# Eight of twelve modulation blocks of a two-layer diffusion step summed on VectorE instead of TensorE

## The chip, the core and the metric

One program on one core of a Trainium2 chip. The metric is the device time of one execution in microseconds (us), here as the median of several runs.

## What is computed

One inference step of a hybrid backbone with two layers over 128 context tokens (stream 0) and 256 latent tokens (stream 1), model width 1024, all in fp32. Per layer and stream (`silu`, `rmsnorm` and `softmax` as usual):

```
mod = silu(c) @ w_mod + b_mod             # 1024 -> 6144; stream 0 uses c_ctx instead of c
sh1, sc1, g1, sh2, sc2, g2 = split(mod, 6)
h = rmsnorm(x) * (1 + sc1) + sh1
z = h @ w_in                              # pooling input, q k v, latent q and kv, 3 x 1024 gates
merged = sum over 3 branches: sigmoid(gate_b) * (y_b @ w_br_b)
x = x + g1 * (merged @ w_out)             # y_b: windowed pooling, windowed GQA, latent attention
h = rmsnorm(x) * (1 + sc2) + sh2
x = x + g2 * moe(h)                       # 16 experts, each takes its top tokens; SwiGLU
```

## The kernel before

Every engine runs a program written out by hand, and semaphores alone tie them together. The 384 tokens are three tiles of 128 (`TILES` = 1, 2, 0). A layer is a mixing part and an expert part.

**Weights.** The mixing weights come as 57 units of 1 MB (`plan_units`), loaded by SyncE in a fixed order through a ring of 8 slots: a unit may be issued once the unit 8 places before it is used up (`wait_mixing`). Each of the 12 modulation blocks `i` (512 columns of `mod`) is two units, the halves of the 1024 rows of `w_mod`. The expert weights come as 96 double units of 2 MB per layer, through the same 8 slots and 8 more (eight doubles in all). The first three doubles go to slots 8 to 13, which lie over memory of the attention, after it (`load_early`, L537 issues every double); the next four wait for the last eight mixing units, and the eighth for the mixed `x`.

**Modulation.** `mod(l, i)` (L1476) is 8 products: the weight operand is `cs`, silu of the two conditions in 32 columns, and 512 columns of `w_mod` stream past; four such products take the four column groups of the array. Their result stands in rows 32q and 32q+1 of a bank and is copied to `modrow` or `g2slot` (`mod_row`, L716). For a block that is needed per channel, `mod_cols` (L1487) adds up the four groups and turns the block into columns by products with a two-column operand; VectorE adds the bias (L1014 to L1019). Blocks 0 to 3 are `sh1` and `sc1`, 4 and 5 `g1`, 6 to 9 `sh2` and `sc2`, 10 and 11 `g2`. `g1` and `g2` are wanted along the rows: one product with a 0/1 matrix spreads them over the partitions (L1737, L1804), and VectorE adds a broadcast bias that GpSimd's queue fetched (`gb`, `g2slot`).

**Mixing part, TensorE's order.** Blocks 0 to 3 and the input projection (L1591, L1627); block 6; transposes of q and k (L1638 to L1653); block 7; the latent query product (L1665) and pooling (L1671); blocks 8 and 9; then for four key tiles `t` the latent key/value product (L1692), and for three of them the transposes of a query tile (L1686); the column products of blocks 6 to 9; the transposes of the four key tiles (L1686); the first scores (L1511 to L1517). VectorE prepares each tile in `query(t)` and `key(t)` (L1214 to L1220); `key(2)` waits for the transposes of key tile 0, `key(3)` for those of tile 1. After `key(2)` VectorE computes amplitude and shift from blocks 6 to 9 and the router's weights (L1237 to L1241).

**Attention.** Eight head pairs `m`. Each turn of the loop on TensorE: `gate` (L1526, 8 products), `branch` (L1545, 4 products), transposes of one head's probabilities (L1554), `gate`, transposes of the other head's, the scores of the next pair, `branch`, `values` (L1566, L1569). ScalarE takes tanh of a gate (L755) and the exponentials; the branch product of the same step takes the gate's bank and so waits for that tanh. VectorE takes the maxima (L1057 to L1066), divides (L1075 to L1079), merges gate and branch (L1044, L1048) and copies (L1251). Then blocks 4 and 5, and eight steps of `gate(2, j)`, `branch(2, j)`.

**Output projection.** `project_out` (L1750) starts once all of `merged` is there; VectorE adds to `x` (`add_mixed`, L1277, L1281); transposes, router, top-k and numbering of tokens follow piece by piece; blocks 10 and 11 stand between the last of them; then the gather (L1815, L1826), evacuated by ScalarE and VectorE (L1388, L1390), the two rows of `g2` (L1804), and the expert part (L1880, L1917) as a loop over four groups of four experts.

## Time and profile before

| | |
|---|---|
| median of 3 runs | 1852.26 us (1850.01 to 1854.09) |
| the profiled execution | 1852.09 us, of which 1850.3 us are its span |
| busy share of the span | TensorE 94%, VectorE 27%, ScalarE 16%, GpSimd 6% |
| chain that ended last | TensorE 73%, DMA 22%, VectorE 2%, ScalarE 1% |
| expert part of layer 0 | 485.7 to about 932 us |
| expert part of layer 1 | 1400.5 us to the end |

A busy TensorE is not TensorE at its peak. The chain is followed back from the last instruction, at each step to what released it; "DMA" in it is time in which the last release was a transfer.

### The profile page before, as it was taken

The page shows a single profiled execution, that of the slowest core. Times are in us where ns is not written, and L with a number is a line of the kernel's source. Part 1 is how long each engine was busy: PE and PEld are TensorE (multiplying, and loading weights), DVE is VectorE, ACT ScalarE, POOL GpSimd, SP SyncE. Part 2 cuts the span into 40 slices and gives each one's busy share as a digit, 9 for nine tenths or more (in the row PEclk, how much of TensorE's full clock was granted, in tenths as well). Part 3 has the DMA queues.
Part 4 walks back from the last instruction along what each step waited for, and adds up shares of the span by engine and source line. Part 5 has one row for each costly group of instructions (what it writes and reads, how often), then busy time and mean ns, then how long its engine had stood idle before and what let it go on. Part 6 is the DMA issues. An engine that isn't in the chain of part 4 may idle for free.

```text
span 1850.3 us, 19029 instructions
## 1 busy us (share of the span) xinstructions
PE 1732.9 (94%) x7336; PEld 806.0 (44%) x7336; DVE 493.6 (27%) x1131; ACT 293.6 (16%) x737; POOL 115.2 (6%) x156
## 2 busy tenths in 40 slices
PE   6998999999999989898899989999999999988987
PEld 3455555554434333242245555555544343323322
DVE  1345333222312211121124344332132221201211
ACT  2233222101201010000022333221012010100100
POOL 1151000000000000000012410000000000000000
PEclk9998999999999999999999989999999999999999
DMA  9452111542999999999983701117419999999997
GB/s 385 182 217 93 69 69 69 207 179 80 381 429 431 431 431 431 431 431 429 428 359 117 278 24 68 69 69 282 172 58 430 429 431 431 431 431 431 430 431 323
DMA packets 48528, 531.77 MB, mean 287 GB/s; under 512 B 5776, under 2 KB 6832, under 8 KB 9808
## 3 DMA queue, kind: packets, MB, share of 16 engines
q1 hardware_dynamic: 45776, 524.45, 68.0%
q0 software_dynamic: 1536, 5.87, 0.9%
q8 instruction: 44, 0.72, 0.2%
q10 hardware_dynamic: 1152, 0.56, 0.1%
q14 instruction: 20, 0.16, 0.0%
HBM read 528.73 MB, written 2.13 MB: 287 GB/s over the span
## 4 chain that ended last, share of the span: by engine, by line
PE 73%; DMA 22%; DVE 2%; ACT 1%; issue 1%; SPq 0%; ACTq 0%; POOL 0%; DVEq 0%; POOLq 0%
PE bank L1880 20%; DMA ring<-in_w_moe 20%; PE bank L1526 13%; PE bank L1545 7%; PE bank L1591 6%; PE bank L1917 5%; PE bank L1750 5%; PE bank L1627 2%; DMA ring<-in_w_mix 2%; PE bank L1476 2%; PE bank L1815 2%; PE bank L1692 2%; PE bank L1554 1%; PE bank L1665 1%; PE bank L1569 1%; PE bank L1514 1%
## 5 line engine op out<-in xcount | busy, mean ns | idle before, releaser
L1526 PE MATMUL bank<-hT,ring 128*128 128x384 f32 x768 | 260.7, 493 | 0.0
L1880 PE MATMUL bank<-M,hT 128*64 128x512 f32 x1024 | 228.8, 595 | 20.4 <-DMA M<-in_w_moe 19.8
L1880 PE MATMUL bank<-ring,hT 128*64 128x512 f32 x1024 | 227.2, 595 | 11.1 <-DMA ring<-in_w_moe 11.1
L1526 PEld LDWEIGHTS bank<-hT,ring 128*128 128x128 f32 x768 | 144.0, 191 | 105.5 <-issue 12.5
L1880 PEld LDWEIGHTS bank<-M,hT 128*64 128x64 f32 x1024 | 73.0, 137 | 168.4 <-issue 137.4
L1545 PE MATMUL bank<-M,ring 128*128 128x384 f32 x384 | 134.2, 492 | 10.1 <-ACT M L755 10.1
L1880 PEld LDWEIGHTS bank<-ring,hT 128*64 128x64 f32 x1024 | 72.7, 137 | 157.5 <-issue 139.2
L1880 PE MATMUL bank<-ring,M 128*64 128x512 f32 x512 | 115.4, 596 | 18.7 <-DMA ring<-in_w_moe 18.7
L1880 PE MATMUL bank<-M 128*64 128x512 f32 x512 | 115.6, 595 | 12.3 <-DMA M<-in_w_moe 12.3
L1591 PE MATMUL bank<-ring,hT 128*128 128x512 f32 (+1 forms) x288 | 117.4, 567 | 2.8 <-DVE hT L1036 2.1
L937 ACT ACTIVATE hT<-bank 128x512 f32<-128x512 f32 x32 | 19.1, 597 | 574.6 <-PE bank L1880 574.6
L1545 PEld LDWEIGHTS bank<-M,ring 128*128 128x128 f32 x384 | 71.0, 190 | 67.9 <-ACT M L755 20.0
L1917 PE MATMUL bank<-M 128*128 128x512 f32 x192 | 93.8, 621 | 3.3 <-DVE M L1413 3.3
L1750 PE MATMUL bank<-ring,xn 128*128 128x512 f32 x192 | 85.5, 596 | 2.3 <-DVE xn L1048 2.3
L1400 DVE SCALAR_TENSOR_TENSOR hT<-hT,bank 128x512 f32<-128x512 f32 x32 | 22.0, 688 | 231.5 <-ACT hT L937 231.5
L1591 PEld LDWEIGHTS bank<-ring,hT 128*128 128x128 f32 x288 | 54.2, 190 | 63.6 <-issue 62.0
L597 POOL TENSOR_TENSOR rstd<-var,mhalf 128x8 f32<-128x8 f32 (+2 forms) x38 | 47.2, 1244 | 515.9 <-DVE var L960 515.8
L1405 DVE SCALAR_TENSOR_TENSOR hT<-hT,bank 128x512 f32<-128x512 f32 x32 | 22.0, 688 | 213.1 <-PE bank L1880 213.1
L1413 DVE TENSOR_TENSOR M<-bank,g2slot 128x512 f32<-128x512 f32 x32 | 22.1, 692 | 210.8 <-PE bank L1880 210.8
L1880 PEld LDWEIGHTS bank<-ring,M 128*64 128x64 f32 x512 | 36.8, 137 | 90.4 <-issue 77.8
L1424 DVE TENSOR_TENSOR x<-x,bank 128x512 f32<-128x512 f32 x96 | 66.0, 688 | 30.2 <-PE bank L1917 30.0
L1880 PEld LDWEIGHTS bank<-M 128*64 128x64 f32 x512 | 37.4, 137 | 83.2 <-issue 79.0
(224 smaller groups left out, 1483.3 us busy)
## 6 DMA issues: line engine op xcount, KB each, us to landing
M<-in_w_moe SPq DMA_DIRECT2D x96, 2048.0 KB, 31.5
ring<-in_w_moe SPq DMA_DIRECT2D x96, 2048.0 KB, 30.6
ring<-in_w_mix SPq DMA_DIRECT2D x110, 1024.0 KB, 7.1
ring<-in_w_mix SPq DMA_DIRECT2D x4, 576.0 KB, 4.5
M<-in_counts POOLq DMA_DIRECT2D x2, 768.0 KB, 12.4
out<-x SPq DMA_DIRECT2D x6, 256.0 KB, 2.0
x<-in_x_sample SPq DMA_DIRECT2D x1, 1024.0 KB, 8.2
M<-in_b_mod POOLq DMA_DIRECT2D x2, 512.0 KB, 7.7
```

The source lines that it names most:

```text
L597: nc.gpsimd.tensor_tensor(rstd[:, c0:c0 + n], var[:, c0:c0 + n], mhalf[:, 0:n], ALU.pow)\
L1424: V.tensor_tensor(xs, xs, bank[b][:, :], ALU.add).then_inc(bank_read[b], 1)
L1476: ins = mm(ps[32 * q:32 * q + 32, :], cs[:, 4 * h + q, :], w[:, q, :], start=(h == 0), stop=(h == 1))
L1526: ins = mm(ps[:, 0:TOK], w[:, q, (j % 4) * P:(j % 4 + 1) * P], hT[:, 4 * h + q, :], start=(h == 0 and q == 0), stop=(h == 1 and q == 3))
L1545: ins = mm(ps[:, 0:TOK], w[:, q, (j % 4) * P:(j % 4 + 1) * P], y[:, q, :], start=(q == 0), stop=(q == 3))
L1591: ins = mm(ps[:, 0:n], hT[:, 4 * h + q, t * P:(t + 1) * P], w[:, q, 0:n], start=(h == 0 and q == 0), stop=(h == 1 and q == 3))
L1627: ins = mm(ps[:, 0:TOK], w[:, q, g * P:(g + 1) * P], hT[:, 4 * h + q, :], start=(h == 0 and q == 0), stop=(h == 1 and q == 3))
L1692: ins = mm(ps[:, :], ckvT[:, k, t * P:(t + 1) * P], w[:, k, h * 512:(h + 1) * 512], start=(k == 0), stop=(k == 1))
L1750: ins = mm(ps[:, :], merged[:, kb, t * P:(t + 1) * P], w[:, kb % 4, :], start=(kb == 0), stop=(kb == 7))
L1815: mm(v[:, :, CP:USED], xn[:, t, kb * P:(kb + 1) * P], gsel[:, t, :].rearrange("p (e s) -> p e s", s=SLOTS)[:, :, CP:USED], start=(t == 1), ...
L1880: ins = mm(bank[b][64 * e:64 * e + 64, :], lhs(e, 4 * h + q), w[:, q, :], start=(h == 0 and q == 0), stop=(h == 1 and q == 3))
L1917: mm(bank[b][:, :], selT[:, t * P:(t + 1) * P], osb[:, n * 512:(n + 1) * 512], start=True, stop=True).then_inc(bank_full[b], 1)
```

## The change

Blocks 6, 7, 8, 9, 4, 5, 10 and 11 (`SUMMED`) are no longer products. VectorE goes over each unit of `w_mod` where it lies in the ring: for each of its four row blocks `q` and each stream `s` it multiplies the 512 columns by `cs[:, kb, s]`, one number per partition, and adds to an accumulator in `modrow` (even blocks) or `g2slot` (odd blocks), 8 instructions per unit and 16 units per layer (`sum_rows`). What is left is the sum over partitions: for blocks 6 to 9 eight products with a single column of ones (`column`, on TensorE), for `g1` and `g2` products of a matrix of ones or of 0/1 slot masks with the accumulators (`modb`, `gate_row`); the bias of these four is loaded into the accumulator beforehand (zero but for partition 0), and VectorE's bias additions and the halving of `g1` move into ScalarE's copy. The four bias loads stand on GpSimd's queue, each behind the product that read the accumulator's last contents; the sum that follows waits for its load. The units stand in a new order, and SyncE waits for `mod_summed` where it waited for a product. The router's weights move into step 1 of the last gate loop. `values(m)` moves behind the first gate of the next pair, except before pair 4. The transposes of the key tiles now follow the last key/value product directly. The output projection waits for `merged` block by block. The mixing part still has 57 units, the expert part is the same.

```diff
 def plan_units():
...
-    for i in (6, 7):
-        units += [("mod", i, 0), ("mod", i, 1)]
-    units += [("wq", 0, 0), ("wq", 1, 0)]
-    for i in (8, 9):
-        units += [("mod", i, 0), ("mod", i, 1)]
-    units += [("wkv", 0, 0)]
...
+    units += [("wq", 0, 0), ("wq", 1, 0), ("wkv", 0, 0)]
+    for b in range(2):
         for h in range(2):
-            units += [("gate", (b, h), 0), ("gate", (b, h), 1), ("br", (b, h), 0)]
-    for n in range(2):
-        units += [("wo", n, 0), ("wo", n, 1)]
-    for i in (10, 11):
-        units += [("mod", i, 0), ("mod", i, 1)]
+            i = 6 + 2 * b + h
+            units += [("mod", i, 0), ("gate", (b, h), 0), ("gate", (b, h), 1), ("br", (b, h), 0), ("mod", i, 1)]
+    units += [("gate", (2, 0), 0), ("gate", (2, 0), 1), ("br", (2, 0), 0), ("mod", 4, 0), ("mod", 4, 1), ("mod", 5, 0),
+              ("gate", (2, 1), 0), ("gate", (2, 1), 1), ("br", (2, 1), 0), ("mod", 5, 1)]
+    units += [("mod", 10, 0), ("mod", 10, 1), ("wo", 0, 0), ("wo", 0, 1), ("mod", 11, 0), ("mod", 11, 1), ("wo", 1, 0),
+              ("wo", 1, 1)]
...
-AFTER_ATTENTION = NU - RING - 1
+AFTER_ATTENTION = UNIT_AT["gate", (2, 1), 1]
...
+SUMMED = (6, 7, 8, 9, 4, 5, 10, 11)
+BIASED = SUMMED[4:]
...
             def wait_mixing(l, u):
 
-                if u in FIRST_AT:
+                if u[0] == "mod" and u[1] in SUMMED:
+                    sp.wait_ge(mod_summed, 2 * len(SUMMED) * l + SUM_AT[u[1], u[2]])
+                elif u in FIRST_AT:
...
-                wait_full(pool, l, ("o", NM - 1))
-                pool.dma_start(gb, a["b_mod"][l, 2 * D:3 * D].partition_broadcast(P)).then_inc(gate_row_in, 16)
-                pool.dma_start(g2slot[:, :], a["b_mod"][l, 5 * D:6 * D].partition_broadcast(P)).then_inc(gate_row_in, 16)
+                for n, i in enumerate(BIASED):
+                    wait_full(pool, l, ("col", 8 + n) if n < 2 else ("modb", BIASED[n - 2], 1))
+                    dst = modrow[:, :, :].rearrange("p s c -> p (s c)") if i % 2 == 0 else g2slot[:, :]
+                    pool.dma_start(dst, a["bias_rows"][l, n]).then_inc(bias_in[n], 16)
...
+                def sum_rows(i, h, qs):
+
+                    u = ("mod", i, h)
+                    w = unit_view(u)
+                    if 0 in qs:
+                        if h == 0 and i in BIASED:
+                            dve.wait_ge(bias_in[BIASED.index(i)], 16 * (l + 1))
+                        dve.wait_ge(*unit_landing(l, u))
+                    for q in qs:
+                        kb = 4 * h + q
+                        for s in range(2):
+                            acc = part_sum(i, s)
+                            if kb:
+                                dve.wait_ge(part_summed, parts[0] - 1)
+                            parts[0] += 1
+                            if kb or i in BIASED:
+                                ins = V.scalar_tensor_tensor(acc, w[:, q, :], cs[:, kb, s:s + 1], acc, ALU.mult, ALU.add)
+                            else:
+                                ins = V.tensor_scalar(acc, w[:, q, :], cs[:, kb, s:s + 1], None, ALU.mult)
+                            ins.then_inc(part_summed, 1)
...
                 for m in range(NM):
                     for j in range(2):
                         divide(l, m, j)
+                    if m in (3, 5, 7):
+                        column(6 + (m - 3) // 2)
                     merge(l, m // 4, 2 * m % 8)
                     for j in range(2):
...
+                        if j == 0:
+                            sum_rows(6 + m // 2, m % 2, (0, 1))
                     if m + 1 < NM:
                         maxima(l, m + 1, 0)
                     merge(l, m // 4, 2 * m % 8 + 1)
                     if m + 1 < NM:
                         maxima(l, m + 1, 1)
+                    sum_rows(6 + m // 2, m % 2, (2, 3))
...
                 for j in range(KB):
                     merge(l, 2, j)
+                    if j == 1:
+                        column(9)
+                        router_weights()
+                    else:
+                        i, h = {0: (4, 0), 2: (4, 1), 3: (5, 0), 4: (5, 1), 6: (10, 0), 7: (10, 1)}.get(j, (0, 0))
+                        if i:
+                            sum_rows(i, h, range(4))
...
                 add_mixed(0, 1)
+                sum_rows(11, 0, (0, 1))
                 add_mixed(1, 1)
+                sum_rows(11, 0, (2, 3))
                 add_mixed(0, 2)
                 turned(1, 1)
                 x_variance(1)
+                sum_rows(11, 1, (0, 1))
                 add_mixed(1, 2)
...
                 affinities(1)
+                sum_rows(11, 1, (2, 3))
                 add_mixed(0, 0)
...
+                def column(i):
+
+                    ps = begin(l, ("col", i))
+                    pe.wait_ge(mod_summed, 2 * len(SUMMED) * l + SUM_AT[i, 1])
+                    for s in range(2):
+                        for c in range(4):
+                            ins = mm(ps[:, 2 * c + s:2 * c + s + 1], part_sum(i, s)[:, c * P:(c + 1) * P], ones[:, 0:1],
+                                     start=True, stop=True)
+                    done(l, ("col", i), ins)
...
                     gate(l, b, j)
+                    if m not in (0, 4):
+                        values(l, m - 1)
+                    if m in (3, 5, 7):
+                        column(6 + (m - 3) // 2)
                     branch(l, b, j)
...
                     branch(l, b, j + 1)
-                    values(l, m)
...
                         if kb % 4 == 0:
                             arrived(l, ("wo", n, kb // 4))
+                        if n == 0 and t == TILES[0]:
+                            pe.wait_ge(merged_ready, 24 * l + 16 + kb + 1)
...
-                pe.wait_ge(merged_ready, 24 * (l + 1))
...
-                mod(l, 10)
+                for k in range(2):
+                    gate_row(10, k)
                 turn_x(0, 1)
-                mod(l, 11, (0,))
+                gate_row(11, 0)
                 router(0)
-                mod(l, 11, (1,))
+                gate_row(11, 1)
...
-                gate_row(10)
-                gate_row(11)
```

Three places of the order, as the program issues them (layer 0).

TensorE, from pooling to the first scores. Before (L1476 the blocks, L1692 the key/value product, L1686 transposes of query and key tiles, L1487 the columns of blocks 6 to 9):

```order
L1671 MATMUL bank<-M 128x384 x4
L1476 MATMUL bank<-ring,cs 32x512 x16
L1692 MATMUL bank<-ring,M 128x512 x4
L1686 MATMUL bank<-const,M 96x128 x8
...
L1692 MATMUL bank<-ring,M 128x512 x4
L1487 MATMUL bank<-const,modrow 128x2 x8
L1487 MATMUL bank<-const,g2slot 128x2 x8
L1686 MATMUL bank<-const,M 96x128 x32
L1511 MATMUL bank<-kT,M 128x128 x2
L1514 MATMUL bank<-kT,M 128x384 x2
```

Of the change (L1725 is L1671, L1744 is L1692, L1738 is L1686, L1567 is L1511):

```order
L1725 MATMUL bank<-M 128x384 x4
L1744 MATMUL bank<-ring,M 128x512 x4
...
L1744 MATMUL bank<-ring,M 128x512 x4
L1738 MATMUL bank<-const,M 96x128 x32
L1567 MATMUL bank<-kT,M 128x128 x2
```

Blocks 8 and 9 and the columns are gone, and the last product is followed by the key transposes.

TensorE, the second head pair. Before (L1526 gate, L1545 branch, L1566 and L1569 values of the first pair):

```order
L1566 MATMUL bank<-M 64x128 x2
L1569 MATMUL bank<-M 64x256 x6
L1526 MATMUL bank<-hT,ring 128x384 x8
L1545 MATMUL bank<-M,ring 128x384 x4
L1554 MATMUL bank<-const,M 128x128 x7
L1526 MATMUL bank<-hT,ring 128x384 x8
```

Of the change (L1582 gate, L1601 branch, L1622 and L1625 values):

```order
L1582 MATMUL bank<-hT,ring 128x384 x8
L1622 MATMUL bank<-M 64x128 x2
L1625 MATMUL bank<-M 64x256 x6
L1601 MATMUL bank<-M,ring 128x384 x4
L1610 MATMUL bank<-const,M 128x128 x7
```

The values of the first pair now stand between the gate of the second pair and its branch.

VectorE, from the last maxima of the second pair to the first copy of transposed probabilities. Before:

```order
L1064 TENSOR_SCALAR negm<-mx,negsink 128x3
L1075 TENSOR_TENSOR esink<-esink,rsum 128x3
L1077 RECIPROCAL rinv<-esink 128x3
L1079 TENSOR_SCALAR M<-M,rinv 128x128
L1079 TENSOR_SCALAR M<-M,rinv 128x384 x2
...
L1044 SCALAR_TENSOR_TENSOR xn<-M,bank 128x384
L1251 COPY M<-bank 128x384 x2
```

Of the change (L1076 is L1064, L1091 is L1079, L1305 is L1251; L1287 is the new sum):

```order
L1076 TENSOR_SCALAR negm<-mx,negsink 128x3
L1287 SCALAR_TENSOR_TENSOR modrow<-ring,cs,modrow 128x512 x4
L1087 TENSOR_TENSOR esink<-esink,rsum 128x3
L1089 RECIPROCAL rinv<-esink 128x3
L1091 TENSOR_SCALAR M<-M,rinv 128x128
L1091 TENSOR_SCALAR M<-M,rinv 128x384 x2
...
L1056 SCALAR_TENSOR_TENSOR xn<-M,bank 128x384
L1305 COPY M<-bank 128x384
L1287 SCALAR_TENSOR_TENSOR modrow<-ring,cs,modrow 128x512 x4
L1305 COPY M<-bank 128x384
```

Four sums of block 6 stand ahead of the division, four more between the two copies.

## Rows read from the trace of the kernel before

**Rows 1.** The chain in order of time: start us, us, what
```profile
485.72 20.82 PE bank L1880 x96
...
883.68 33.36 DMA ring<-in_w_moe
...
1400.50 20.82 PE bank L1880 x96
...
1798.58 33.36 DMA ring<-in_w_moe
```

**Rows 2.** SyncE's queue, four expert loads around the first expert product
```profile
473.35 23.25 SPq L537 DMA_DIRECT2D M<-in_w_moe  x4
```

**Rows 3.** ScalarE in order of time, layer 0: start us, us, instruction [idle before]
```profile
111.51 0.38 ACT L798 ACTIVATE M<-bank 128x256 f32<-128x256 f32 x1
113.08 0.60 ACT L716 ACTIVATE modrow<-bank 128x512 f32<-128x512 f32 x1 [1.19 <-PE bank L1476]
```

**Rows 4.** TensorE in order of time: three places of layer 0
```profile
133.74 3.64 PE L1476 MATMUL bank<-ring,cs 128*32 128x512 f32 x32
...
382.08 5.32 PE L1526 MATMUL bank<-hT,ring 128*128 128x384 f32 x16
...
389.82 5.32 PE L1526 MATMUL bank<-hT,ring 128*128 128x384 f32 x16
```

**Rows 5.** The chain: transposes behind the key projections, layers 0 and 1
```profile
155.46 3.47 PE bank L1487 x32
...
1071.14 4.04 PE bank L1487 x32
```

**Rows 6.** TensorE in order of time: first scores of layers 0 and 1
```profile
170.35 0.80 PE L1511 MATMUL bank<-kT,M 64*128 64x128 f32 x4 [0.88 <-ACT M L851]
...
1086.85 0.80 PE L1511 MATMUL bank<-kT,M 64*128 64x128 f32 x4 [0.88 <-ACT M L851]
```

**Rows 7.** VectorE in order of time, the third key tile of layer 0
```profile
156.90 0.17 DVE L960 TENSOR_SCALAR var<-ss 128x8 f32<-128x8 f32 x1
160.54 0.88 DVE L1214 TENSOR_TENSOR M<-bank,rstd 128x256 f32<-128x256 f32 x2 [3.47 <-PE bank L1686]
...
162.18 0.42 DVE L1220 TENSOR_TENSOR M<-krg,rstd 128x256 f32<-128x256 f32 x1
```

**Rows 8.** Stretch of 2 us, TensorE alone: busy, granted clock, DMA share, GB/s
```profile
171.00:173.00 2.00, 2.00 (x10) 0.50 0.00 0
```

**Rows 9.** TensorE in order of time, from the second head pair to the third
```profile
217.03 1.47 PE L1569 MATMUL bank<-M 128*64 128x256 f32 x12
...
224.43 2.85 PE L1545 MATMUL bank<-M,ring 128*128 128x384 f32 x8 [0.58 <-ACT M L755]
...
227.12 0.93 PE L1554 MATMUL bank<-const,M 128*128 128x128 f32 x7
```

**Rows 10.** TensorE at the start and the end of the output projection's stage
```profile
422.24 7.99 PE L1750 MATMUL bank<-ring,xn 128*128 128x512 f32 x18 [1.16 <-DVE xn L1048]
...
483.50 1.94 PE L1804 MATMUL bank<-modrow,const 128*128 128x512 f32 x4
```

**Rows 11.** VectorE in order of time, before the last tile's output projection
```profile
458.08 0.23 DVE L1316 TENSOR_SCALAR M<-M 128x16 f32<-128x16 f32 x1
...
459.62 0.69 DVE L1277 TENSOR_TENSOR M<-bank,M 128x512 f32<-128x512 f32 x1 [1.30 <-PE bank L1750]
```

**Rows 12.** VectorE, the last gathered rows before the experts of layer 0
```profile
484.86 0.40 DVE L1390 TENSOR_SCALAR hT<-bank,amp,shift 128x128 f32<-128x128 f32 x1
```

**Rows 13.** Groups by line and shape: instructions, busy us, mean ns, idle before
```profile
L1281 DVE TENSOR_TENSOR x<-x,M 128x512 f32<-128x512 f32 x12 | 8.3, 692 | 0.4
```

**Rows 14.** VectorE in order of time, between the second and third head pair
```profile
219.86 0.23 DVE L1064 TENSOR_SCALAR negm<-mx,negsink 128x3 f32<-128x3 f32 x1
...
220.40 0.95 DVE L1079 TENSOR_SCALAR M<-M,rinv 128x128 f32<-128x128 f32 x3
```

**Rows 15.** DMA issues by line: KB each, median us to landing
```profile
g2slot<-in_b_mod POOLq DMA_DIRECT2D x1, 512.0 KB, 11.2
```

More of the change, by code:

```diff
@@ L245 @@
 LANDS = [c + (12 * NP // ND if s % 2 == 0 else 0) for s, c in enumerate(LANDED)]
-FIRSTS = [u for u in UNITS if u[2] == 0 and u[0] in ("mod", "seg", "gate", "wo")]
+SUMMED = (6, 7, 8, 9, 4, 5, 10, 11)
+BIASED = SUMMED[4:]
+SUM_AT = {(i, h): 2 * n + h + 1 for n, i in enumerate(SUMMED) for h in range(2)}
+FIRSTS = [u for u in UNITS if u[2] == 0 and u[0] in ("mod", "seg", "gate", "wo") and not (u[0] == "mod" and u[1] in SUMMED)]
 FIRST_AT = {u: n for n, u in enumerate(FIRSTS)}
@@ L501, in row_of, with part_sum, unit_landing @@
         def row_of(i):
-            return g2slot[:, (i - 8) * 512:(i - 7) * 512] if i in (8, 9) else modrow[:, MODROW[i], :]
+            return modrow[:, MODROW[i], :]
+        def part_sum(i, s):
+            return modrow[:, s, :] if i % 2 == 0 else g2slot[:, s * 512:(s + 1) * 512]
+        def unit_landing(l, u):
+            s = slot_of(u)
+            before = sum(slot_of(v) == s for v in UNITS[:UNIT_AT[u]])
+            return landed[s], 16 * (l * LANDS[s] + before + 1)
         def unit_view(u, width=512):
@@ L1465, in arrived, with mod @@
             def arrived(l, u):
-                s = slot_of(u)
-                before = sum(slot_of(v) == s for v in UNITS[:UNIT_AT[u]])
-                pe.wait_ge(landed[s], 16 * (l * LANDS[s] + before + 1))
-            def mod(l, i, halves=(0, 1)):
-                ps = begin(l, ("mod", i)) if 0 in halves else bank[turn(l, ("mod", i))[0]]
-                for h in halves:
+                pe.wait_ge(*unit_landing(l, u))
+            def mod(l, i):
+                ps = begin(l, ("mod", i))
+                for h in range(2):
                     arrived(l, ("mod", i, h))
@@ L1696, in _ @@
                         turn_heads("tqm", t, t)
-                begin(l, ("modcol", 1))
-                for i in range(6, 10):
-                    mod_cols(l, 1, i, i - 6, i == 9)
                 for t in range(4):
@@ L1725, in _ @@
                     branch(l, b, j + 1)
-                    values(l, m)
-                for i in (4, 5):
-                    mod(l, i)
+                values(l, NM - 1)
                 for j in range(KB):
@@ L1732, in _ @@
                     branch(l, 2, j)
-                    if j < 2:
-                        wait_read(pe, l, ("mod", 4 + j))
+                    if j == 0:
+                        column(9)
+                    if j in (3, 6):
+                        i = 3 + j // 3
+                        pe.wait_ge(mod_summed, 2 * len(SUMMED) * l + SUM_AT[i, 1])
                         for v in range(2):
-                            ps = begin(l, ("modb", 4 + j, v))
-                            done(l, ("modb", 4 + j, v), mm(ps[:, :], pick[v], modrow[:, j, :], start=True, stop=True))
+                            ps = begin(l, ("modb", i, v))
+                            done(l, ("modb", i, v), mm(ps[:, :], ones, part_sum(i, v), start=True, stop=True))
                 ps = begin(l, ("rcon", 0))
@@ L2001 @@
     arrays["w_moe"] = expert_units(v)
+    rows = np.zeros((L, len(BIASED), P, 2, 512), np.float32)
+    for n, i in enumerate(BIASED):
+        rows[:, n, 0] = v["b_mod"][:, None, i * 512:(i + 1) * 512]
+    arrays["bias_rows"] = rows.reshape(L, len(BIASED), P, D)
     def columns(a, n):
```

145 lines of the change are left out of this document (73 added, 72 removed).

## The prediction

> **What bounds the kernel now.** I read the chain of waits first. In the expert part of either layer it begins with products and then turns into waits for expert weights; the last of these ends 431.3 us (layer 0) and 431.4 us (layer 1) after the layer's first expert product [rows 1]. So the expert part is a stream of transfers whose length is fixed from its own first product on. Can the stream begin earlier without TensorE? Only eight double units fit. In SyncE's queue the eighth is the first of four issued from 473.35 us [rows 2], before the first expert product at 485.72 us [rows 1]; the ninth needs a slot that only expert products free. The 88 doubles behind it follow TensorE's start. **So the time moves by exactly what the change takes off the mixing parts up to the first expert product, once per layer.** The mixing part I read next as TensorE's timeline, where it is busy almost throughout, and its idle times are what ScalarE and VectorE end. VectorE is idle most of the mixing part; the sums are to live there.
>
> **The terms, per layer.** W is the end of the last key/value product.
>
> 1. Block 6 stands between the projection and the transposes. What comes next is bound by ScalarE: its last copy of the pooling input ends at 111.51 + 0.38 = 111.89 us, and it then waits for block 6 and copies it until 113.08 + 0.60 = 113.68 us [rows 3] before it can go on to DMA issues and the copies that the latent query product waits for. Gain 1.8 us. Block 7 stands inside that same wait and counts nothing.
> 2. Blocks 8 and 9 stand on TensorE's path, VectorE being done with what the next product needs: 3.64 us [rows 4]. The units of the next products arrive earlier than before, since four units fewer are ahead of them.
> 3. The column products of blocks 6 to 9 and what follows. Before, from W = 155.46 to the first scores at 170.35 us it is 14.9 us; in layer 1, from 1071.14 to 1086.85, 15.7 us [rows 5, 6]. After: VectorE's statistics of key tile 3 end 156.90 + 0.17 - 155.46 = 1.6 us behind W. Then `key(2)`, which no longer has to stand 3.47 us for TensorE, takes from 160.54 to 162.18 + 0.42, that is 2.1 us [rows 7], `key(3)` as much (the router's weights that stood between them, about 3 us, are gone), the last tile's transposes 1.0 to 1.9 us, and the scores wait for ScalarE's copy 0.88 us [rows 6]. Together 7.7 to 8.6; I take 8.2. Gain 6.7 us in layer 0, 7.5 in layer 1.
> 4. Attention. The branch stands 0.58 us for ScalarE's tanh in each turn [rows 9]. With `values` (1.47 us, same rows) in between, the tanh is done: 6 x 0.58 = 3.5 us in the six turns where it is moved. Against it stand three `column` groups. The nearest row is the old column products, 32 records in 3.47 us [rows 5], so 16 records are 1.74 us; bounds 0.9 us (if one column costs half of two) and 2.0 us (layer 1's 4.04 us, partly at half clock). Cost 5.2, net a loss of 1.7 us.
> 5. Blocks 4 and 5 as 8 and 9: a gain of 3.64, less the fourth `column`, 1.74: 1.9 us.
> 6. The output projection stood 1.16 us for the last merge [rows 10]. Now only its eighth product needs that merge, 6 us later. Gain 1.2 us. (SyncE's wo unit of the second half is freed with the last branch product and has 7 us to land.)
> 7. Blocks 10 and 11 give way to four 512-column products in the same places, 3.7 us against 3.5: nothing, the chain there runs over VectorE and ScalarE. VectorE now has four sums between the affinities that end at 458.31 and `add_mixed` at 459.62 us [rows 11]; four take 2.9 us (below), so that addition is some 1.2 us late, but TensorE wants it only at 462 us: a loss of 0.3 us.
> 8. The two `g2` products ran to 483.50 + 1.94 = 485.44 us [rows 10] ahead of the experts, but VectorE's last gathered rows end at 484.86 + 0.40 = 485.26 us anyway [rows 12], so only 0.3 us are won.
>
> Sum: 1.8 + 3.6 + 6.7 - 1.7 + 1.9 + 1.2 - 0.3 + 0.3 = **13.5 us in layer 0**, 14.3 in layer 1, 27.8 together. Against the profiled execution's 1852.09 us, which lies 0.2 below the median, that is 1824.3; from the median, 1824.4 us.
>
> A rule against term 4's size: the old column products show 0.108 us per record [rows 5]. The Trainium skill (TensorE: Matmul & The Clock Gate, Back-to-back issue gap) gives matmuls of up to 64 columns some 25 ns; by that four groups would cost 1.6 us and not 7, and the time be about 1813 us. The trace speaks for its other rule, in LDWEIGHTS, that a weight load costs its number of columns, 107 ns at 128: each of these products has its own load.
>
> **What VectorE's 128 sums are covered by.** No row has a multiply-add from SBUF of this shape; a two-input one of 512 columns takes 0.692 us [rows 13], 0.72 with its gap. Lower bound 0.5 (one input), upper bound twice the row. Four before the division: the last maxima end at 219.86 + 0.23, the division of the first head (0.95 us and its two small ones, [rows 14]) then starts 2.9 us later and ends near 224.4; TensorE wants that head at 227.12, with the stall gone at 226.5 us [rows 9]. Slack 2 us. The four behind the first copy end two microseconds before the second copy. In the last loop a step is 389.82 - 382.08 = 7.74 us [rows 4], merge and eight sums 1.2 + 5.8 = 7.0: hidden, with 0.7 us to spare, more since every second operation waits only for the one before the last. If the cover fails there, each step costs what it is over, after a lag of about one step that the two tanh buffers allow. ScalarE loses eight copies and gains as many.
>
> **Rivals.**
>
> *The clock falls behind the columns* (6%). The stretch of small transposes and column products before the scores ran at the lower level, 1.2 GHz [rows 8]; one-column products are as small. If TensorE ran at half clock for 4 us behind each of eight groups, 2 us each, 16 us come back: 1840 us. Against it: the same 16-record groups in the first blocks of the layer show no fall.
>
> *The clock stays up before the scores* (10%). With less waiting, the last transposes and scores could run at 2.4 GHz: some 2.2 us less per layer, 1820 us.
>
> *VectorE's key chain or the attention slack is tighter than worked out* (12%). Then term 3 gives little more than the columns' 3.5 us, or the sums push the division: 3 to 4 us less per layer, 1832 us.
>
> *The expert stream does move on its own* (3%). The first ring slots come free some 30 us earlier, and if that counted, the stream would gain one or two doubles per layer, 5 to 8 us: about 1810 us. Against it is the limit of eight.
>
> *The bias loads come late; slower than before* (4%). The sum of block 4 waits for its load on GpSimd's queue, and on VectorE everything stands behind it: merges, then TensorE's next gates. The old load of this size landed in 11.2 us [rows 15]. From issue to need there are about 23 us for block 4, 24 for 5 and 10 (three steps of 7.74 and a merge), and 16 for block 11. At 34 us, three times the row, they would be 11, 10, 10 and 18 us late, 49 per layer against 14 gained: 1922 us. It decides from about 26 us on. The Trainium skill (SBUF — State Buffer, Who interferes with whom) has a mechanism for it: VectorE operations in a two-port mode keep GpSimd from writing descriptors for its own queue. The row speaks against: the old loads were issued amid divisions and merges.
>
> **How the numbers follow.** My forecast case (65%) covers 1820 to 1829 us: the bounds of the columns (-7 to +2 us), half a microsecond each way in term 3, and layer 0's gather, which ran partly at half clock and may or may not. To leave out no more than a fifth the range takes in the full clock and the tighter chain: 1817 to 1836 us. A measurement of this kernel tells about 0.2%, 3.7 us, from no change. All cases but the bias loads gain more: faster 0.94, same 0.02, slower 0.04.
>
> **What would show it.** Last expert wait to first expert product still 431 us in both layers; W to first scores near 8 us; no 0.58 us before the branch in turns 1 to 3 and 5 to 7; four groups of 1.7 us for the columns; 0.7 us or less per sum; bias landing under 16 us; projection starting without its 1.16 us. The prediction is wrong if the span from first expert product to last wait changes, or if TensorE waits in the last gate loop.

## The result and the profile after

| | before | after |
|---|---|---|
| median | 1854.09 us (1850.01 to 1855.86, 5 runs) | 1839.39 us (1837.74 to 1845.11, 5 runs) |
| span of the profiled execution | 1850.3 us | 1837.6 us |

The ratio is 0.9932, with a 95% interval of 0.9911 to 0.9953: faster by 0.7%. The forecast of 1824.4 us (range 1817 to 1836) missed it; 12.7 us of span were won, not 27.8. One execution of the last experiment below, `c3`, took 1920.03 us at a granted clock of 0.90 and is left out of its ratio.

**The lock.** The chain of the changed kernel, both layers (start us, us, what); it answers to [rows 1]:

```profile
478.00 22.52 PE bank L1948 x96
...
877.81 33.35 DMA ring<-in_w_moe
...
1386.16 22.52 PE bank L1948 x96
...
1785.87 33.36 DMA ring<-in_w_moe
```

From the first expert product to the end of the last wait it is 433.2 and 433.1 us, 1.8 and 1.6 more than before. (The `x96` in these rows counts records of the profile. An fp32 product leaves two of them, so these are 48 products.) The stream's length did stay tied to TensorE, but its first 96 records take 22.52 us and not 20.82. The first product comes only 7.7 us earlier in layer 0, where 13.5 were forecast.

**Up to the first branch.** TensorE in order of time, layer 0 (start us, us, instruction, count, [idle before]); the first line is the latent query product, 36 records:

```profile
117.76 13.34 PE L1719 MATMUL bank<-ring,M 128*128 128x384 f32 x36 [3.03 <-ACT M L816]
...
159.52 0.49 PE L1567 MATMUL bank<-kT,M 64*128 64x128 f32 x4 [0.93 <-ACT M L851]
...
168.47 2.85 PE L1601 MATMUL bank<-M,ring 128*128 128x384 f32 x8 [1.80 <-ACT M L759]
```

The same product before, and the granted clock (the number after the busy time and its count) at it, before and after:

```profile
118.99 11.85 PE L1665 MATMUL bank<-ring,M 128*128 128x384 f32 x36 [0.30 <-issue]
```
```profile
118.00:120.00 2.00, 1.70 (x11) 1.00 0.98 346
120.00:122.00 2.00, 2.00 (x8) 1.00 1.04 406
```
```profile
118.00:120.00 2.00, 2.00 (x4) 0.50 0.03 8
120.00:122.00 2.00, 2.00 (x7) 0.81 0.00 0
```

The product starts 1.2 us earlier and then loses 1.5 us, part of it at a granted clock of 0.50, which is 1.2 GHz: TensorE had stood idle for 3.03 us just before. Before the change, block 7 (1.93 us) filled most of that wait. In the chain the last key/value product is `148.42 3.45 PE bank L1744 x8`, so W is 151.87 and the scores follow 7.65 us behind it. They now run at 2.4 GHz (granted clock 1.00 from 157 to 161 us), unlike [rows 8]. The scores and the first gate together take 2.8 us less, but only 1.6 of it arrives at the first branch: its wait for ScalarE is 1.80 us, where it was 0.58.

**Attention.** TensorE, turns 2 to 5 of layer 0 (L1582 gate, L1601 branch, L1764 column):

```profile
205.13 5.43 PE L1582 MATMUL bank<-hT,ring 128*128 128x384 f32 x16 [0.65 <-DVE xn L1056]
...
212.16 2.85 PE L1601 MATMUL bank<-M,ring 128*128 128x384 f32 x8
...
227.18 5.40 PE L1582 MATMUL bank<-hT,ring 128*128 128x384 f32 x16 [0.84 <-DVE xn L1056]
...
234.17 1.95 PE L1764 MATMUL bank<-const,modrow 128*128 128x1 f32 x16
...
258.92 2.85 PE L1601 MATMUL bank<-M,ring 128*128 128x384 f32 x8 [0.58 <-ACT M L759]
...
274.86 5.43 PE L1582 MATMUL bank<-hT,ring 128*128 128x384 f32 x16 [0.65 <-DVE M L1056]
```

The 0.58 us ahead of the branch [rows 9] are gone in the six turns where the values moved; in turn 4, where they did not, the wait is still there (the row at 258.92). A new wait stands ahead of the gate, for VectorE's merge (L1056). There are six per layer: five of 0.65 and one of 0.84, 4.1 us.

**The end of the mixing part.** TensorE, layer 0 (L1832 turned `x`, L1850 last route, L1885 gather, L1948 experts), and the clock around the first expert product:

```profile
453.27 0.63 PE L1832 MATMUL bank<-const,x 128*128 128x128 f32 x4 [0.48 <-DVE x L1338]
...
465.61 0.40 PE L1850 MATMUL bank<-const,M 128*128 128x16 f32 x2 [1.41 <-ACT g2slot L926]
...
468.57 4.54 PE L1885 MATMUL bank<-M,xn 128*128 128x128 f32 x24 [0.35 <-DVE M L1404]
...
478.00 12.22 PE L1948 MATMUL bank<-M,hT 128*64 128x512 f32 x48 [1.91 <-DVE hT L1451]
```
```profile
479.00:481.00 2.00, 2.00 (x8) 0.54 0.00 0
481.00:483.00 2.00, 2.00 (x8) 0.60 0.00 0
```

In layer 1 the end of the mixing part before, and then after:

```profile
1392.65 2.92 PE L1815 MATMUL bank<-M,xn 128*128 128x128 f32 x24 [0.35 <-DVE M L1347]
...
1400.50 10.52 PE L1880 MATMUL bank<-M,hT 128*64 128x512 f32 x48 [0.18 <-issue]
```
```profile
1376.70 4.54 PE L1885 MATMUL bank<-M,xn 128*128 128x128 f32 x24 [0.35 <-DVE M L1404]
...
1386.16 12.22 PE L1948 MATMUL bank<-M,hT 128*64 128x512 f32 x48 [1.94 <-DVE hT L1451]
```

The wait for a turned `x` is VectorE's four sums, and the 1.41 us end with ScalarE's copies of the `g2` rows. What follows the longer idle times runs in part at half clock: in layer 1 the 24 records of the gather take 4.54 instead of 2.92 us, and in both layers the first 48 records of the experts take 12.22 instead of 10.52. The gather of layer 0 was slow before the change as well:

```profile
476.14 4.54 PE L1815 MATMUL bank<-M,xn 128*128 128x128 f32 x24 [0.35 <-DVE M L1347]
```

So one slow gather in two before stands against two in two after; what the change did to the gather rests on more runs, given below.

**The account**, in us won from stretch to stretch, each the difference of two starts in the two traces:

| stretch (term) | forecast, layers 0 / 1 | measured |
|---|---|---|
| start of the trace up to the projection | 0 / 0 | -0.3 / 0 |
| to the query product (1) | 1.8 / 1.8 | 1.5 / 1.6 |
| query product | 0 / 0 | -1.5 / 0 |
| pooling, blocks 8 and 9 (2), to W | 3.6 / 3.6 | 3.9 / 3.9 |
| W to the scores (3) | 6.7 / 7.5 | 7.2 / 8.0 |
| scores to the first branch | 0 / 0 | 1.6 / 1.6 |
| first branch to the output projection (4, 5, 6) | 1.4 / 1.4 | -3.2 / -3.2 |
| output projection to the gather (7) | -0.3 / -0.3 | -1.7 / -1.8 |
| gather to the first expert product (8) | 0.3 / 0.3 | 0.2 / -1.6 |
| expert part | 0 / 0 | -1.8 / -1.6 |
| sum (from unrounded times) | 13.5 / 14.3 | 5.9 / 6.8 |

### The profile page after: what moved, and what is told of

Read it like the earlier page. It is cut to its first block, busy times and chain, and to the rows that moved or that the text cites. A ratio compares the mean times of both kernels' runs of the same rounds, so it can differ in the third digit from the quotient of the medians.

```text
span 1837.6 us, 18931 instructions
## 1 busy us (share of the span) xinstructions
PE 1710.4 (93%) x7152; PEld 804.0 (44%) x7152; DVE 651.5 (35%) x1381; ACT 290.3 (16%) x733; POOL 118.2 (6%) x160
## 4 chain that ended last, share of the span: by engine, by line
PE 72%; DMA 22%; DVE 3%; ACT 1%; issue 1%; SPq 0%; ACTq 0%; POOL 0%; DVEq 0%; POOLq 0%
PE bank L1948 21%; DMA ring<-in_w_moe 20%; PE bank L1582 13%; PE bank L1601 7%; PE bank L1647 6%; PE bank L1985 5%; PE bank L1818 4%; PE bank L1683 2%; DMA ring<-in_w_mix 2%; PE bank L1885 2%; PE bank L1744 2%; PE bank L1719 1%; PE bank L1610 1%; PE bank L1625 1%; PE bank L1570 1%
## 5 line engine op out<-in xcount | busy, mean ns | idle before, releaser
L1582 PE MATMUL bank<-hT,ring 128*128 128x384 f32 x768 | 259.2, 491 | 8.2 <-DVE xn L1056 4.3
L1948 PE MATMUL bank<-M,hT 128*64 128x512 f32 x1024 | 232.2, 603 | 23.7 <-DMA M<-in_w_moe 19.8
L1948 PE MATMUL bank<-ring,hT 128*64 128x512 f32 x1024 | 227.2, 595 | 11.2 <-DMA ring<-in_w_moe 11.2
L1582 PEld LDWEIGHTS bank<-hT,ring 128*128 128x128 f32 x768 | 143.0, 190 | 113.4 <-DVE M L1056 8.3
L1948 PEld LDWEIGHTS bank<-M,hT 128*64 128x64 f32 x1024 | 73.7, 138 | 172.8 <-issue 141.8
L1948 PEld LDWEIGHTS bank<-ring,hT 128*64 128x64 f32 x1024 | 72.6, 137 | 157.7 <-issue 139.3
L1601 PE MATMUL bank<-M,ring 128*128 128x384 f32 x384 | 134.0, 492 | 4.8 <-ACT M L759 4.8
L1948 PE MATMUL bank<-ring,M 128*64 128x512 f32 x512 | 115.4, 596 | 18.7 <-DMA ring<-in_w_moe 18.7
L1948 PE MATMUL bank<-M 128*64 128x512 f32 x512 | 115.9, 596 | 12.3 <-DMA M<-in_w_moe 12.3
L1601 PEld LDWEIGHTS bank<-M,ring 128*128 128x128 f32 x384 | 71.0, 190 | 57.5 <-ACT M L759 7.2
L1287 DVE SCALAR_TENSOR_TENSOR g2slot<-ring,cs,g2slot 128x512 f32<-128x512 f32 x120 | 81.9, 746 | 0.4
L1287 DVE SCALAR_TENSOR_TENSOR modrow<-ring,cs,modrow 128x512 f32<-128x512 f32 x120 | 81.5, 746 | 0.3
L1948 PEld LDWEIGHTS bank<-ring,M 128*64 128x64 f32 x512 | 36.8, 137 | 90.4 <-issue 77.8
```

What stands on the lines that cost most here:

```text
L1287: ins = V.scalar_tensor_tensor(acc, w[:, q, :], cs[:, kb, s:s + 1], acc, ALU.mult, ALU.add)
L1582: ins = mm(ps[:, 0:TOK], w[:, q, (j % 4) * P:(j % 4 + 1) * P], hT[:, 4 * h + q, :], start=(h == 0 and q == 0), stop=(h == 1 and q == 3))
L1601: ins = mm(ps[:, 0:TOK], w[:, q, (j % 4) * P:(j % 4 + 1) * P], y[:, q, :], start=(q == 0), stop=(q == 3))
L1948: ins = mm(bank[b][64 * e:64 * e + 64, :], lhs(e, 4 * h + q), w[:, q, :], start=(h == 0 and q == 0), stop=(h == 1 and q == 3))
```

## The experiments

All are edits of the changed kernel, and their line numbers are shifted by a few against it. Where two spans are compared below, the stretch from first branch to first expert product (layer 0) is given as well, since chance in the clock ahead of it does not reach it: 309.5 us in the changed kernel.

**Which order of the values costs what.** My theory: gate and branch share one bank, so a gate right behind a branch waits for its merge, and a branch right behind a gate waits for its tanh; one piece of work can cover only one of them. The rival: the sums make VectorE late. `e1` (e1_values_split) puts four of the eight value products ahead of the gate and four behind it:

```diff
+                    if m not in (0, 4):
+                        values(l, m - 1, ("first",))
                     gate(l, b, j)
                     if m not in (0, 4):
-                        values(l, m - 1)
+                        values(l, m - 1, ("second",))
```

> Against the changed kernel: the eight value products of turns 1 to 3 and 5 to 7 are cut in two, four of them (0.65 us) ahead of the gate group and four (0.86 us) behind it. Theory A (moving values behind the gate uncovered the merge of the last branch, which reads the one bank that gate and branch share: waits of 0.65, 0.65, 0.84, 0.65, 0.65, 0.65 us = 4.09 us per layer; and what stands behind the gate hides the tanh): both waits are gone, 8.2 us over two layers, 1839.4 - 8.2 = 1831.2 us; first expert product to last expert wait stays 433.1 us. Theory B (VectorE is late in general, with the sums in its queue): the wait moves to the value products or stays, 1839.4 within 1.5 us.

Measured: 1832.53 us (1830.77 to 1837.29), ratio to before 0.9891 (0.9874 to 0.9908), span 1830.7. TensorE in turn 2:

```profile
203.90 0.44 PE L1623 MATMUL bank<-M 128*64 128x128 f32 x4
204.17 0.60 PE L1628 MATMUL bank<-M 128*64 128x256 f32 x4
204.70 5.43 PE L1582 MATMUL bank<-hT,ring 128*128 128x384 f32 x16
210.06 1.08 PE L1628 MATMUL bank<-M 128*64 128x256 f32 x8
211.07 2.85 PE L1601 MATMUL bank<-M,ring 128*128 128x384 f32 x8
```

No wait is left at any of the twelve gates. The stretch is 306.0 us, 3.5 less and not 4.1: the two halves take 0.80 and 1.01 us, up to what follows each, against 1.67 in one piece, which is 0.14 us in each of six turns and more than covers the 0.6 missing. `e2` (e2_values_back) puts all values ahead of the gate again:

> Against the changed kernel: the value products stand ahead of the gate again, as before the change. Theory A (each place of the values hides one wait and uncovers the other): the six merge waits (4.09 us per layer) go, the six tanh waits of 0.58 us (3.48) return: 1839.4 - 1.2 = 1838.2 us. Theory B (the merge wait is VectorE's backlog from the sums and not the order): the merge waits stay in some form and the tanh waits are added, about 1839.4 + 7 = 1846 us.

Measured: 1836.91 us (1835.75 to 1837.73), ratio 0.9908 (0.9893 to 0.9922), span 1835.1. The merge waits go and only three tanh waits of 0.58 us return, in turns 1, 2 and 6: in 3, 5 and 7 the column group stands between gate and branch and covers it, which the expectation overlooked. The stretch is 306.4 us, 3.1 less than in the changed kernel. So for this kernel the old place was better than the new one, and cutting the values in two is only 0.4 us per layer better than putting them back (first branch to output projection, 240.8 against 241.3 us in both layers). Of the 4.4 us between the spans of `e1` and `e2`, 3.8 lie outside the two stretches; the largest piece is the query product of layer 1, 11.85 against 13.54 us. `e4` (e4_two_sums) leaves 14 of 16 sums out:

```diff
                         kb = 4 * h + q
+                        if kb:
+                            continue
```

> Leaves out 14 of the 16 sums of each block, so the modulation is not computed. Against the changed kernel, Theory A (the sums are hidden but for four of block 11 ahead of the last front addition: a wait of 0.48 us per layer, and 0.2 us of the 0.84 us merge wait of turn 3): 1.4 us less, 1838 us; six merge waits of 0.65 us remain. Theory B (the sums are what makes VectorE late in the attention and the projection): the merge waits go, 4 us per layer and more, below 1832 us.

Measured: 1840.16 us (1837.29 to 1841.2), span 1838.0: nothing won. All twelve merge waits are there unchanged, 0.84 included, so the rival falls: the sums left out, 14 of 16, had cost the attention nothing. The 0.48 us ahead of the turned `x` are gone, but the gather (L1887) gave them back:

```profile
468.03 5.29 PE L1887 MATMUL bank<-M,xn 128*128 128x128 f32 x24 [0.25 <-DVE M L1406]
...
478.31 10.52 PE L1950 MATMUL bank<-M,hT 128*64 128x512 f32 x48 [2.01 <-DVE hT L1453]
```

The 24 records of the gather now take 5.29 us, and the experts of this layer stayed at the upper level in spite of 2.01 us of idle time. Over the seven runs in which nothing fills the waits ahead of the gather (the changed kernel twice, `e1`, `e2`, `e4` to `e6`) the gather took 4.4 to 5.4 us in all 14 layers. In the six of them that also leave the wait ahead of the experts empty (all but `e6`), the first 48 records of the experts took 12.22 us in 11 layers of 12; this is the twelfth.

**Whether the removed products had kept the clock up.** Products with ones, into a bank nobody reads, in TensorE's idle times:

```diff
+                wait_read(pe, l, ("tq", 0))
+                for k in range(6):
+                    mm(bank[5][:, :], ones, const[:, 0:512], start=True, stop=True)
                 for t in range(T):
                     wait_read(pe, l, ("tkc", t))
```

and likewise 2, 4 and 4 (then 1, 2 and 2) ahead of the last route, of the last turned affinities and of the first expert product (e3_kept_busy; with three, one, two and two, e3b_kept_busy_less).

> Against the changed kernel: products with ones of 512 columns (0.43 us each), whose results nobody reads, stand in four idle stretches of TensorE: six ahead of the latent query products (idle 3.03 and 2.86 us), two and four around the last route (idle 1.41 and 1.7 to 1.9 us), four ahead of the first expert product (idle 1.91 and 1.94 us). Theory A (the removed blocks and gate products had kept TensorE at 2.4 GHz; it falls to 1.2 GHz behind the idle time): the query products of layer 0 return from 13.34 to 11.85 us, the gather's 24 products from 4.54 to 2.92 us, the first 96 expert products from 22.52 to 20.8 us: 1.5 + 2 x (1.6 + 1.7) = 8.1 us less, 1831.3 us, and first expert product to last expert wait 431.4 us again. Theory B (the clock there falls for another reason): granted clock as in the changed kernel, time the same or up to 1 us longer, 433 us of expert part.

Measured: 1841.66 us (1840.15 to 1843.59). TensorE (L1942 is the filling):

```profile
477.95 3.65 PE L1942 MATMUL bank<-const 128*128 128x512 f32 x8
481.53 10.52 PE L1957 MATMUL bank<-M,hT 128*64 128x512 f32 x48
```

A miss of mine: one product of this type is two records of 0.43 us, so four of them are eight records and 3.5 us, twice the wait. The granted clock was 1.00 at every filled place in both layers (it fell once elsewhere, to a mean of 0.91 from 1065 to 1085 us), but it was paid for. With half as many:

> The run before showed a filling product to be two records of 0.43 us, so that its stretches were twice as long as meant. Now three, one, two and two of them: 2.6 us into the idle 3.0 before the query products, 0.9 into 1.4, 1.7 into 1.7 and 1.7 into 1.9 us at the end of the mixing part. Against the changed kernel, Theory A (half clock behind idle time, which the removed products had filled): 1.5 us in layer 0's query products, 1.6 in each gather, 1.7 at each start of the experts: 8.1 us less, 1831.3 us; expert part 431.5 us. Theory B (the clock gives back nothing on the path): 1839.4 within 1 us though the clock is full.

Measured: 1832.25 us (1830.86 to 1834.59), ratio 0.9878 (0.9862 to 0.9894), span 1831.0:

```profile
117.69 11.85 PE L1722 MATMUL bank<-ring,M 128*128 128x384 f32 x36 [0.36 <-issue]
...
468.71 2.92 PE L1888 MATMUL bank<-M,xn 128*128 128x128 f32 x24 [0.32 <-issue]
...
476.62 10.52 PE L1957 MATMUL bank<-M,hT 128*64 128x512 f32 x48 [0.24 <-issue]
```

In the chain the last expert wait of layer 0 ends at 874.48 + 33.36 = 907.84: the expert part is 431.2 us again. In both layers the query product takes 11.85, the gather 2.92 and the first 48 records of the experts 10.52 us. Useless work made the kernel 7 us faster.

**The columns** (e5_one_column).

```diff
-                    for s in range(2):
-                        for c in range(4):
-                            ins = mm(ps[:, 2 * c + s:2 * c + s + 1], part_sum(i, s)[:, c * P:(c + 1) * P], ones[:, 0:1],
-                                     start=True, stop=True)
+                    ins = mm(ps[:, 0:8], part_sum(i, 0)[:, 0:P], ones[:, 0:8], start=True, stop=True)
```

> Each column group is one product with eight columns of ones instead of eight with one column, so the second modulation's shift and amplitude are wrong. Theory A (a group of 16 records takes 1.8 us and all of it is on TensorE's path): 1.6 us less for each of four groups and two layers, 12.9 us, 1826.5 us. Theory B (groups partly cover waits: those of turns 3, 5 and 7 stand ahead of a branch that waits for its tanh, and the merge behind it would be late): 1 to 2 us of each layer's 6.4 come back as waits, 1829 to 1831 us.

Measured: 1832.95 us (1830.81 to 1833.35), span 1829.0, 8.6 us less than the changed kernel's, where theory A said 12.9. The stretch from first branch to first expert product is 303.3 us in layer 0, 6.2 less than with the columns (6.3 in layer 1), close to theory A (6.4), and the waits in it are unchanged. The times of the whole kernel would not have told this: ahead of the stretches the run lost about 4 us. The query product took 13.54 us in both layers (13.34 and 11.85 in the changed kernel) and started 0.9 us later in layer 0, and layer 1 took 1.4 us longer from the scores to the first branch.

**The copies on the way to the router.** `e6` (e6_rows_split) puts block 11's two row products ahead of the experts and both copies behind ScalarE's part of the gathered inputs:

```diff
-                for i in (11, 10):
-                    ps = wait_full(act, l, ("modb", i, 0))
-                    read(l, ("modb", i, 0), F(g2slot[:, (i - 10) * 512:(i - 9) * 512], ps[:, :], ACT.Copy))
...
                 gathered(0)
+                for i in (11, 10):
+                    ps = wait_full(act, l, ("modb", i, 0))
+                    read(l, ("modb", i, 0), F(g2slot[:, (i - 10) * 512:(i - 9) * 512], ps[:, :], ACT.Copy))
```

> Against the changed kernel: block 11's two row products (1.7 us) go behind the gather, in front of the first expert product, as the old ones stood; ScalarE's two copies of the rows (1.0 us) go behind its part of the gathered inputs. Theory A: TensorE's wait of 1.41 us for the router falls to some 0.3, and the 1.91 us ahead of the experts are filled, so that the first 96 expert products take 20.8 instead of 22.5 us: 1.1 + 1.7 = 2.8 us per layer, 1833.8 us; expert part 431.5 us. Theory B (VectorE's selection is as late as the router): only the clock's 1.7 us per layer, 1836 us.

Measured: 1837.37 us (1836.8 to 1838.51), span 1834.9, 2.7 less, where theory A said 5.6. Up to 1.7 us of the shortfall is the query product of layer 1, 13.54 us in this run and 11.85 in the changed kernel's. The stretch is 309.1 us, 0.4 less, and the expert part 431.3, 1.9 less: 2.3 us in layer 0 and 2.1 in layer 1, where theory A said 2.8. The first 48 records of the experts take 10.52 us in both layers, so the two row products do there what filling does. But the gather takes 5.3 to 5.4 us: with the row products taken from between its small steps, TensorE idled there for 4.0 us in five waits, against 3.5 in three,

```profile
462.26 0.65 PE L1842 MATMUL bank<-hT,wrA 128*32 128x128 f32 x16 [0.73 <-ACT hT L892]
463.51 0.37 PE L1850 MATMUL bank<-const,M 128*128 128x16 f32 x2 [0.60 <-ACT M L898]
464.95 0.26 PE L1865 MATMUL bank<-const,M 16*128 16x16 f32 x2 [1.08 <-DVE M L1392]
466.55 0.37 PE L1857 MATMUL bank<-const,M 128*16 128x128 f32 x1 [1.34 <-DVE M L1373]
467.17 5.33 PE L1885 MATMUL bank<-M,xn 128*128 128x128 f32 x24 [0.24 <-DVE M L1404]
```

so 0.8 us of what the experts won was lost again one stage up.

**Together** (c1_all).

> All mends at once on the changed kernel: values split in two, block 11's rows and both copies late, block 11's last four sums behind the first turned inputs, three filling products ahead of the query products and one ahead of the gather, and the first column group in turn 4, where the branch still waits 0.58 us. Theory A (the parts add): -7.0 -5.6 -1.0 -1.5 -3.2 -1.2 = -19.5, 1820 us. Theory B (what is won at the end of the mixing part is given back by the gather, at half clock as soon as TensorE idles): 3 to 4 us less of it, 1823 to 1824 us.

Measured: 1825.06 us (1822.57 to 1825.16), ratio 0.9834 (0.982 to 0.9847): nearer to theory B. The granted clock was 0.54 from 462 to 466 us, in spite of the one filling product ahead of the gather, and the gather took 4.0 us. The next runs leave the row products in their place and move the copies alone.

> The changed kernel once more, as the measure for the two runs beside it: 1839.4 us within 1.5. If the granted clock behind the idle 3 us ahead of the latent query products is a matter of chance, their 36 records take 11.85 us in some layers and 13.3 to 13.5 in others.

> Against the changed kernel: values split in two; the row products stay where they are and ScalarE's two copies of them go behind the gathered inputs; three filling products (0.86 us each) ahead of the query products, one and one around the turned slots, two ahead of the experts; first column group in turn 4. Theory A (measured parts: values 7.0, fillings 6.9, column 1.2; the copies take 1.0 us out of ScalarE's chain to the router per layer): 17.1 us less, 1822.3 us. Theory B (the chain over VectorE, whose selection ends some 0.3 us behind the router product, takes the copies' place, and a filling product that is longer than its wait costs): 1824 to 1825 us, no better than all mends at once.

> The same, with one filling product each in the waits of 1.25, 0.9 and 0.93 us of the last key tiles and the first scores and half a one in that of 0.51 us. Theory A (the level there falls by chance, as in two runs of eight layers, where scores begin 0.7 us later): 0 to 1.5 us less than the run beside it. Theory B (a filling product delays the transposes behind it more than the clock gives back): 0.5 to 1.5 us more.

Measured: the changed kernel 1841.27 us (1838.2 to 1842.24, ratio 0.9929 where it was 0.9932), 0.4 above the range expected for it; `c2` 1822.1 us (1820.68 to 1825.08, ratio 0.9836, 0.9824 to 0.9849), `c3` 1821.18 us (ratio 0.9826, 0.9813 to 0.9839). The end of the mixing part in `c2`:

```profile
460.76 0.27 PE L1871 MATMUL bank<-const,M 128*16 128x128 f32 x1 [0.18 <-DVE M L1374]
461.38 2.92 PE L1899 MATMUL bank<-M,xn 128*128 128x128 f32 x24 [0.35 <-DVE M L1405]
469.29 10.52 PE L1967 MATMUL bank<-M,hT 128*64 128x512 f32 x48 [0.24 <-issue]
```

The stretch is 302.4 us in layer 0, 7.1 less than in the changed kernel: 3.5 from the values (`e1`), 1.5 from the fillings (308.0 us in `e3b`), 0.9 from the column group's place (first branch to output projection, 240.0 us against 240.8 in `e1`) and 1.2 from the copies (output projection to experts, 62.4 us against 63.6 in `e3b`). The 1.41 us ahead of the last route are gone. The last two parts are differences between runs and were not tried alone. `c2` came out at theory A's 1822.3. `c3` cannot be told from it, so whether filling the waits of the last key tiles gains anything stays open. Both beat both kernels, the old one by 1.6 and 1.7%, the changed one by 1%. In the repeat of the changed kernel the query product took 13.42 and 13.54 us. Over all seven runs that share the code there (it twice, `e1`, `e2`, `e4` to `e6`) it took 13.3 to 13.5 us in layer 0 every time, and in layer 1 twice 11.85 and five times 13.5: 1.7 of the 2.8 us between the two spans of the changed kernel (1837.6 and 1840.4). In the five runs with filling products ahead of it, it took 11.8 to 11.9 us in all ten layers.

## Why the prediction was wrong

- **What bounds the kernel** was right: in every run the last expert wait moved with the first expert product. The size was right only at full clock: 431.2 to 431.6 us in every layer whose experts begin at 2.4 GHz (`e3`, `e3b`, `e6`, `c1` to `c3`, layer 0 of `e4`), 432.9 to 433.2 in every other layer of the changed kernel and its edits. By the prediction's own last line, a changed span from first expert product to last wait makes it wrong. "Exactly what the change takes off" left out that TensorE's state at that point is carried over, 1.7 us per layer.
- **Term 1** (1.8 us): the start moved by 1.5 and 1.6 us, a little less than forecast, since ScalarE's DMA issues had begun at 113.09 us and not behind the end of its copy at 113.68. That block 7 "counts nothing" failed: it had filled 1.9 us of TensorE's wait, and behind the empty 3 us the query product lost 1.5 us in layer 0. `e3b` shows it: with filling in that wait the loss is gone.
- **Terms 2 and 3** held, 3.9 and 3.9, 7.2 and 8.0 us. The rival *the clock stays up before the scores*, given 10%, came true as well, with 1.6 us per layer and not 2.2, and it hid part of the miss. It is not certain in every layer: of the 14 layers of the seven runs, 11 take 8.9 us from the scores to the first branch and three 10.2 to 10.3. Why the level fell there before the change and mostly stays up now was not tested.
- **Term 4** is the step that failed most: it priced the move of `values` by the 3.5 us of tanh waits that it takes away and put only the columns against it; the merge waits that it opened are 4.1 us per layer. That with `values` in between "the tanh is done" is true, but I did not ask what the values had covered at their old place. I named what a moved step would hide and not what it had been hiding. The columns were sized right: 1.8 us each in the trace, 1.55 for seven eighths of one (`e5`). A rule of the Trainium skill (TensorE: Matmul & The Clock Gate, LDWEIGHTS) that the time of a weight load goes by its number of columns fits that. The page's 25 ns for a narrow matmul (Back-to-back issue gap) is a floor that these groups stay far above, with some 110 ns per record.
- **Terms 5 and 6** held within what the attention's stretch can tell: it fell short of the forecast by 4.6 us, and the merge waits are 4.1 of them. The 1.16 us ahead of the output projection are gone. The last gate loop has no wait, so the sums fit in it: four take 2.65 us.
- **Term 7** (-0.3): -1.7 and -1.8. The wait of 0.48 us for the sums was foreseen at 0.3; by the prediction's own rows the addition is late by 2.9 less the 1.30 us of idle time, 1.6 us, and not 1.2. ScalarE "loses eight copies and gains as many", but not in the same places: two of the new ones now stand on the way to the router, take 1.08 us and end the wait of 1.41 us. Moving them gave 1.2 us per layer in `c2`, as a difference between runs.
- **Term 8** (+0.3): removing the two `g2` products was costed by VectorE's end alone. They had kept TensorE busy for the 1.9 us in which the gathered rows are evacuated. Without them the clock fell within the first records of the experts in 11 layers of 12, at 1.7 us each. `e3b` (filling) and `e6` (two row products put back there) both show it: 10.52 us in both layers.
- **The rival *the clock falls behind the columns*** had the right kind of loss at the wrong place: in the trace of the changed kernel the clock was 1.00 in the 8 to 9 us from the start of each of the eight groups; it fell behind idle time elsewhere, most of which the change opened. *The bias loads come late* did not happen: they landed in 5.8 and 7.3 us (median).

The account misses the forecast by 15.1 us: 8.2 are merge waits, 1.5 the query product, 2.0 the stretch from gather to experts, 3.4 the experts' slow start, 2.9 the stage of the output projection; term 3 and the scores gave 4.2 back, and 1.3 are spread over the other rows. Of the 2.0, 1.6 are layer 1's gather; layer 0's was as slow before, which the prediction had left open in its range.

The Trainium skill (TensorE: Matmul & The Clock Gate, Part 1: The HAM clock gate) says that the level follows how busy TensorE has been, and that the count of slow products varies between runs of one kernel; the 11.85 and 13.54 us that the same query product took in layer 1 agree.

## What to carry to other kernels

When a piece of work is moved into a wait, look up what it was covering where it stood: where a shared bank has a wait on both sides, moving the work swaps one wait for the other. Cutting it in two removed both, though here it gained only 0.4 us per layer over leaving it in its old place, because the column groups covered three of the other waits there. Work that TensorE does in a wait is not free to remove if what follows then runs at 1.2 GHz; cost a removal by the idle time that it opens and by the records behind it at both levels. A stream locked to its first product carries a slow start to its end. When single layers differ by 1.7 us from run to run, compare two kernels over a stretch of the trace that the chance does not reach.

## What the runs showed of the hardware

The granted clock fell to 0.50 behind waits that I had costed by their length alone, and mostly but not always: behind 2.9 to 3.8 us of idle time the query product lost 1.5 to 1.7 us in 12 layers of 14, and behind 1.9 to 2.1 us the experts lost 1.7 us in 11 layers of 12. Work that does nothing kept it at 1.00 at these two places in every layer that had it: 2.6 us of it or more ahead of the query product (`e3`, `e3b`, `c1` to `c3`, ten layers), 1.7 us or more ahead of the experts (`e3`, `e3b`, `c2`, `c3`, eight layers). One filling product ahead of the gather in `c1` did not: the clock was 0.54 there. One fp32 product of 512 columns is two records of 0.43 us; I had read a record as a product.
